# Fixed slots for the weight blocks, and another order of rounding, in the Strassen sets of an encoder's MLP

## What is computed

```python
h = _layer_norm(ALPHA * h + (mix @ w_out + b_out), ln1_g, ln1_b)
f = jnp.square(jax.nn.relu(h @ w_mlp1 + b_mlp1)) @ w_mlp2 + b_mlp2
h = _layer_norm(ALPHA * h + f, ln2_g, ln2_b)
```

## Time and profile before

| | us |
|---|---|
| median of 3 runs | 799.43 (797.58 to 800.34) |
| the profiled execution, its own time | 798.34 |
| its span | 796.6 |
| TensorE busy | 776.4 (97%) |
| VectorE busy | 519.6 (65%) |
| ScalarE busy | 426.8 (54%) |
| GpSimd busy | 145.9 (18%) |
| mean granted TensorE clock | 0.994 |

### The profile page before, as it was taken

One profiled execution on the slowest core, in us unless ns is written; L12 is line 12 of the kernel. 1 busy time (PEld: TensorE's weight loads), 2 busy tenths in 40 slices (PEclk: granted clock), 3 DMA queues, 4 the chain that ended last, 5 costly groups with the idle time before them and its releaser, 6 DMA issues.

```text
span 796.6 us, 14048 instructions
## 1 busy us (share of the span) xinstructions
PE 776.4 (97%) x5720; PEld 748.6 (94%) x5720; DVE 519.6 (65%) x762; ACT 426.8 (54%) x666; POOL 145.9 (18%) x195
## 2 busy tenths in 40 slices
PE   8999999999999999999999999999999999999995
PEld 7999899999989999999999999998999999999994
DVE  6823344754546476876968979687775887655644
ACT  5633345655646465563655556587336763477324
POOL 2100000472220110006640000000000000000356
PEclk9999999999999999999999999999999999999998
DMA  8632131112111112233112366645666456653203
GB/s 313 261 123 95 58 114 53 54 57 81 53 53 54 53 53 73 88 114 125 58 50 80 80 190 176 163 123 143 186 173 171 130 141 175 173 125 133 80 2 119
DMA packets 27070, 90.57 MB, mean 114 GB/s; under 512 B 2864, under 2 KB 7104, under 8 KB 26624
## 3 DMA queue, kind: packets, MB, share of 16 engines
q1 hardware_dynamic: 22592, 74.26, 27.3%
q0 software_dynamic: 4000, 15.10, 10.3%
q10 hardware_dynamic: 416, 0.33, 0.1%
HBM read 84.84 MB, written 4.85 MB: 113 GB/s over the span
## 4 chain that ended last, share of the span: by engine, by line
PE 80%; DVE 7%; ACT 6%; issue 3%; DMA 3%; DVEq 0%; ACTq 0%; POOL 0%; SPq 0%; POOLq 0%
PE lin L751 8%; PE lin L752 8%; PE lin L753 8%; PE z L1268 6%; PE z L1269 6%; PE z L1270 6%; PE z L1007 3%; DMA raw<-w_sets 3%; PE lin L1145 3%; PE lin L1146 3%; PE lin L1147 3%; PE lin L1285 2%; PE lin L1287 2%; PE lin L1286 2%; PE lin L1268 2%
## 5 line engine op out<-in xcount | busy, mean ns | idle before, releaser
L751 PE MATMUL lin<-h_hi,whi 128*128 128x288 f32 (+1 forms) x448 | 133.8, 299 | 0.0
L752 PE MATMUL lin<-h_lo,whi 128*128 128x288 f32 (+1 forms) x448 | 132.5, 296 | 0.0
L753 PE MATMUL lin<-h_hi,wlo 128*128 128x288 f32 (+1 forms) x448 | 132.0, 295 | 0.0
L751 PEld LDWEIGHTS lin<-h_hi,whi 128*128 128x128 f32 x448 | 84.2, 188 | 1.3 <-issue 1.1
L752 PEld LDWEIGHTS lin<-h_lo,whi 128*128 128x128 f32 x448 | 84.2, 188 | 0.1
L753 PEld LDWEIGHTS lin<-h_hi,wlo 128*128 128x128 f32 x448 | 84.3, 188 | 0.0
L1839 ACT ACTIVATE whi<-raw 128x1024 fp32r<-128x1024 f32 x48 | 50.7, 1056 | 55.4 <-DMA raw<-w_sets 18.0
L2695 DVE TENSOR_TENSOR wlo<-raw,whi 128x1024 fp32r<-128x1024 f32 x48 | 58.7, 1223 | 22.3 <-ACT whi L1839 22.3
L2098 DVE TENSOR_TENSOR wlo<-raw,whi 128x1024 fp32r<-128x1024 f32 x41 | 50.9, 1242 | 28.6 <-ACT whi L1361 26.5
L1361 ACT ACTIVATE whi<-raw 128x1024 fp32r<-128x1024 f32 x38 | 40.0, 1053 | 50.5 <-PE lin L753 32.5
L1268 PE MATMUL z<-f_ops,whi 128*128 128x288 f32 x176 | 52.8, 300 | 3.4 <-DVE f_ops L2764 2.0
(11 more groups left out here) (456 smaller groups left out, 2572.7 us busy)
## 6 DMA issues: line engine op xcount, KB each, us to landing
raw<-w_stream SPq DMA_DIRECT2D x64, 512.0 KB, 3.2
raw<-w_sets SPq DMA_DIRECT2D x48, 512.0 KB, 3.6
raw<-w_sets POOLq DMA_DIRECT2D x24, 512.0 KB, 6.9
w_fifth<-w_sets SPq DMA_DIRECT2D x12, 512.0 KB, 6.2
r<-x_t SPq DMA_DIRECT2D x8, 296.0 KB, 4.4
kcache<-k_cache SPq DMA_DIRECT2D x1, 2048.0 KB, 9.8
vcache<-v_cache SPq DMA_DIRECT2D x1, 2048.0 KB, 8.0
y<-r SPq DMA_DIRECT2D x8, 160.0 KB, 1.8
```

The lines of the kernel that those rows point to most:

```text
L751: pe.matmul(out, w_h, hi, start=first, stop=False)
L752: pe.matmul(out, w_h, lo, start=False, stop=False)
L753: return pe.matmul(out, w_l, hi, start=False, stop=last)
```

## The change

The slots no longer alternate: a, b, c, d, g are always 1, 3, 0, 2, 4. The next set's SI base goes into SI's slot as soon as SI's low part and X are made, AP's base into AP's slot behind AP's low part, AL behind DP's sum (which reads X in that slot), DE behind DP's low part, GA as before.

DP's sum moves from s2 to s3 (behind the third sum and ahead of `op_lo` of DP). ScalarE rounds V5 ahead of the next set's SI instead of behind it, and rounds B21 and T3 at s1 and V4 at s3 of the set behind, where before it rounded B21 at s0 and T3 and V4 at s1. VectorE takes V5's low part at s6 of the in set, ahead of the next set's X; V4's sum goes behind the low part of X; the low part of B21 is taken at s1, of T3 at s2, and of B22 and V4 at s4, where before B21 and T3 were at s1, B22 at s2 and V4 at s3. The low part of B11 or C11 goes behind `op_lo` at s5. In set 0 the residual operations move from s0 to s3 to s1, s2, s4 and s5.

```diff
-def set_slots(t):
-    return (1, 3, 0, 2, 4) if t % 2 == 0 else (0, 2, 1, 3, 4)
+def set_slots():
+    return 1, 3, 0, 2, 4
...
             for t in range(1, N_SETS):
-                a, b, c, d, g = set_slots(t)
+                a, b, c, d, g = set_slots()
                 o = OPS * (t - 1)
                 sp.wait_ge(s_lo, o + W_SI + 1)
                 sp.wait_ge(x_made, t)
-                load_block(t, a, 0, al_in)
-                sp.wait_ge(s_lo, o + W_X + 1)
-                sp.wait_ge(dp_made, t)
                 load_block(t, c, 2, si_base)
                 sp.wait_ge(s_lo, o + W_AP + 1)
+                load_block(t, d, 2, ap_base)
+                sp.wait_ge(dp_made, t)
+                load_block(t, a, 0, al_in)
+                sp.wait_ge(s_lo, o + W_DP + 1)
                 load_block(t, b, 1, de_in)
-                sp.wait_ge(s_lo, o + W_DP + 1)
-                load_block(t, d, 2, ap_base)
                 sp.wait_ge(s_lo, o + W_GA + 1)
                 load_block(t, g, 3, ga_in)
...
                 elif p < 3:
-                    v_hi(t, T3)
-                    v_hi(t, V4)
+                    for o in {1: (B21, T3), 3: (V4,)}.get(s, ()):
+                        v_hi(t, o)
...
                         op_hi(o + 2)
                         if SETS[tail][1] < 3:
                             v_hi(tail, V6)
-                            v_hi(tail, B21)
                         continue
...
                             block_hi(t, C12)
                         block_plain(t, C12)
+                        if p < 3:
+                            v_hi(t, V5)
                     op_hi(o + s + 2)
...
-                    if s == 1 and tail is not None:
-                        set_tail(tail, 1)
+                    if s and tail is not None:
+                        set_tail(tail, s)
...
-                    if kind == "in" and s == 6 and p < 3:
-                        v_hi(t, V5)
-                    if t == 0 and s < 4:
-                        residual2((4, 0, 2, 6)[s])
-                        residual2((5, 1, 3, 7)[s])
+                    if t == 0 and s in (1, 2, 4, 5):
+                        m = {1: 4, 2: 0, 4: 2, 5: 6}[s]
+                        residual2(m)
+                        residual2(m + 1)
...
                         if blocks:
                             last_lo(tail, C12)
-                        if sums:
-                            set_lo(tail, V5)
-                            v_sum(tail, V4)
                     if inner:
                         if s == 3:
                             third_sum(t)
                         elif s == 5:
                             fourth_sum(t)
-                            last_lo(t, C11) if p == 3 else set_lo(t, B11)
+                        elif s == 6 and p < 3:
+                            v_sum(t, V5)
+                            v_sum(t, T3)
                     elif s >= 2:
                         out_add(t, s - 2)
-                    if s == 6 and inner and p < 3:
-                        v_sum(t, V5)
-                        v_sum(t, T3)
-                    if s == 2:
+                    if s == 3:
                         dp_sum(t)
                     op_lo(o + s + 2)
...
                     if sums:
-                        for f in {0: (V6,), 1: (B21, T3), 2: (B22,), 3: (V4,)}.get(s, ()):
+                        if s == 0:
+                            v_sum(tail, V4)
+                        for f in {0: (V6,), 1: (B21,), 2: (T3,), 4: (B22, V4)}.get(s, ()):
                             set_lo(tail, f)
                     if blocks and s == 0:
                         last_lo(tail, C21)
+                    if inner and s == 5:
+                        last_lo(t, C11) if p == 3 else set_lo(t, B11)
...
                         else:
                             v_sum(t, V6)
+                            set_lo(t, V5)
                     if s == 6:
                         x_sum(t + 1)
```

More of the change, by code:

```diff
@@ L68, in sets_before, with source_slot @@
     return sum(k == kind for k, _, _ in SETS[:t])
-def set_slots(t):
-    return (1, 3, 0, 2, 4) if t % 2 == 0 else (0, 2, 1, 3, 4)
-def source_slot(t, s):
-    a, b, c, d, g = set_slots(t)
+def set_slots():
+    return 1, 3, 0, 2, 4
+def source_slot(s):
+    a, b, c, d, g = set_slots()
     return (a, c, a, b, d, b, g)[s]
@@ L689, in _ @@
             sp.wait_ge(lo_split, U_MLP1 + HIDDEN - 3)
-            load_block(0, set_slots(0)[2], 2, si_base)
+            load_block(0, set_slots()[2], 2, si_base)
             sp.wait_ge(lo_split, U_MLP1 + HIDDEN - 2)
-            load_block(0, set_slots(0)[0], 0, al_in)
+            load_block(0, set_slots()[0], 0, al_in)
             sp.wait_ge(lo_split, U_MLP1 + HIDDEN - 1)
-            load_block(0, set_slots(0)[3], 2, ap_base)
+            load_block(0, set_slots()[3], 2, ap_base)
             sp.wait_ge(lo_split, U_MLP1 + HIDDEN)
-            load_block(0, set_slots(0)[1], 1, de_in)
+            load_block(0, set_slots()[1], 1, de_in)
             sp.wait_ge(f_lo_done, F_TILES)
-            load_block(0, set_slots(0)[4], 3, ga_in)
+            load_block(0, set_slots()[4], 3, ga_in)
             for t in range(1, N_SETS):
-                a, b, c, d, g = set_slots(t)
+                a, b, c, d, g = set_slots()
                 o = OPS * (t - 1)
@@ L1838, in op_hi @@
                     act.wait_ge(op_done, o - 2)
-                nc.scalar.activation(op_home(o)[0], set_home(source_slot(t, s)), ACT.Copy).then_inc(s_hi, 1)
+                nc.scalar.activation(op_home(o)[0], set_home(source_slot(s)), ACT.Copy).then_inc(s_hi, 1)
             def first_copy(t):
@@ L2678, in x_sum @@
                     return
-                a, _, c, _, _ = set_slots(t)
+                a, _, c, _, _ = set_slots()
                 dve.wait_ge(si_in, 16 * (t + 1))
@@ L2683, in dp_sum @@
             def dp_sum(t):
-                a, b, _, _, _ = set_slots(t)
+                a, b, _, _, _ = set_slots()
                 dve.wait_ge(x_made, t + 1)
@@ L2694, in op_lo @@
                 dve.wait_ge(s_hi, o + 1)
-                tt(home[1], set_home(source_slot(t, s)), home[0].bitcast(F32), ALU.subtract).then_inc(s_lo, 1)
+                tt(home[1], set_home(source_slot(s)), home[0].bitcast(F32), ALU.subtract).then_inc(s_lo, 1)
             def out_add(t, n):
@@ L3200, in _ @@
             for t in range(N_SETS):
-                _, _, c, d, _ = set_slots(t)
+                _, _, c, d, _ = set_slots()
                 pool.wait_ge(si_base, SET_IN + 16 * (t + 1))
```

## The result

The changed kernel takes 811.91 us (811.58 to 813.04, 4 runs) against 798.96 us: a ratio of 1.0165, with an interval of 1.0144 to 1.0186. It is 13 us slower. The forecast was 809.9 us, in a range of 804 to 815. The profiled execution takes 811.58 us, its span is 809.9 us, 13.3 us more than before.

The account below looks back on a forecast made before the run. TensorE, busy for 97% of the span, was taken to bound the kernel, so only its idle time and slower stretches could change. Terms of +4.6, +6.7 and -0.8 gave +10.5 us, hence 809.9 us, range 804 to 815.

Parts of the forecast that it names:

- The sum: Whole kernel: +4.6 us for sets 2 to 5, +6.7 for sets 6 to 9, -0.8 for set 0, +10.5 us.
- Set 0: With residual operations no longer ahead of ScalarE's copy, s2 starts at 461.04 and not 461.88: 0.84 us won.
- The stalls: TensorE waits in sets 3 and 4, and likewise 7 and 8: 0.15, 1.56, 2.37, 2.38, 1.57 and 1.39 us.
- VectorE being late at s3: Set 3: lateness at s3 gives the part of the 2.4 us s6 wait above 0.6 us.
- the low end of my range: 804 us: VectorE in time at set 3's s3 saves 3.5 us in two places, smaller waits 2 us less together.
- Two of the signs: TensorE's waits for sums' low parts in sets 4 and 8 exceed 9 us; ScalarE's waits for blocks nearly vanish.
- The clock: Falls of TensorE's granted clock behind stalls in sets 3, 4, 7 and 8: taken as 0, upper end 3.4 us.
- a fall there costs nothing, since TensorE then waits anyway: Behind s6 of set 3 or s1 of set 4, a clock fall is covered by waits of 2.4 or 1.6 us.
- the 3.4 us that I had set beside it: Upper end for clock falls behind the 1.35 us stall at s5, 1.7 us each in two places.
- AL: AL, loaded behind DP's sum, lands 4 us after issue; in set 2 ScalarE wants it 4.5 us after that sum.
- Rival 2: AL lands late, at 8.8 us, delaying C22 blocks: 14 us on top, 824; chance 0.07 for more than 6 us landing.
- Rival 1: The SI block held the chain; without it sums are in time: 790.3 us, or 795 for set 4 alone; chance 0.10.

Follow-up runs that it names:

- e10: Changed kernel with the low parts of B22 and V4 moved behind the fourth sum in sets 3 and 7: 808.26 us.
- e5: Changed kernel with ScalarE's rounding of V5 put back behind the rounding of the next set's SI: 806.76 us.
- e3: Changed kernel with DP's sum put back at s2, ahead of AP's low part: 803.71 us.
- e9: Changed kernel with the base of SI for set 1 loaded ahead of GA of set 0: 810.92 us.
- e6: Changed kernel with V5's low part back behind X and V4's sum back ahead of X's low part: 811.06 us.
- e1: Kernel before with only the fixed slots and loads of the change, old order on VectorE and ScalarE: 796.25 us.
- e7: Rework of the changed kernel: slots kept, SI of set 1 early, DP's sum at s2, V5's rounding behind SI's, several low parts and sums moved: 792.33 us.
- e4: Changed kernel with the low part of B22 back at s2 and that of V4 back at s3: 806.58 us.
- e2: Changed kernel with the old alternating slots and loads, new order on VectorE and ScalarE kept: 816.32 us.

## Why the prediction was right

**The sum.** 10.5 us were forecast and 13 measured, with an interval of 11.5 to 14.9. For sets 2 to 5 and 6 to 9 the forecast was 76.6 us each; measured 76.64 and 76.60. Set 0 was to win 0.84 us and won 0.7.

**The stalls.** At s2 of set 3, 1.56 forecast and 1.52 measured (as distance between matmuls over 0.133 us); at s6, 2.37 and 2.35; at s1 of set 4, 2.38 and 2.41; at s5, 1.39 and 1.37. At s4 of set 3 none was forecast and none came. e10 and e5 confirm two of the parts of which they were made: 1.3 us for two low parts, 1.1 us for the order of V5's and SI's rounding.

The stall at s6 of set 3 had its size right and its parts wrong. I had put 0.6 us of it down to the new order there and the rest to VectorE being late at s3. In e5 TensorE waits 0.9 us less at s2 and the stall at s6 is still 2.35 us; from s2 to s6 it is 15.22 us (530.62 to 545.84), in the changed kernel 15.23 (531.97 to 547.20). So the lateness of set 3's start gives nothing of it, and the 3.5 us that it took off for the low end of my range are a saving that no run shows. What e3 and e10 show in its place is DP's sum at s3, without which there is no stall at all, and on top of it the two low parts.

Two of the signs came only in part. TensorE's waits for the sums' low parts grew to 6.9 us and not to over 9, since a fall of the clock filled the time of the wait at s2 of sets 4 and 8 (below). And ScalarE's waits for blocks fell from 24.6 to 7.9 us, but that for SI of set 1 (4.5 us) stayed, which points at the set that I left out.

**The clock.** A fall came behind s1 of sets 4 and 8, none at s6. At s2 of set 4, where 1.57 us of stall were forecast, the changed kernel shows 0.04: the fall took the stall's place. e3, which has a stall of 2.4 us at s1 as well but no fall, shows what that place costs without one:

```profile
552.56 0.37 PE L1267 MATMUL z<-f_ops,whi 128*128 128x288 f32 x1 [2.23 <-DVE f_ops L2763]
...
557.39 0.37 PE L1267 MATMUL lin<-f_ops,third_hi 128*128 128x288 f32 x1 [1.44 <-DVE f_ops L2763]
```

4.83 us from s1 to s2 in e3, 4.82 in the changed kernel (556.05 to 560.87). e10 has both in one execution: behind s1 of set 4 no fall and behind s1 of set 8 one (the column ahead of the last two), and the sets take 27.68 and 27.71 us.

```profile
555.50:558.50 3.00, 2.87 (x22) 2.64 (x21) 1.87 (x3) 2.50 (x4) 0.00 (x0) 1.00 0.50 164
...
653.50:656.50 3.00, 3.00 (x15) 3.00 (x14) 2.15 (x3) 3.00 (x5) 0.00 (x0) 0.50 0.54 175
```

So the step "a fall there costs nothing, since TensorE then waits anyway" holds. It holds for s6 too: in e9 the clock falls behind s6 of sets 3 and 7, and the pairs take 54.3 and 54.2 us, as in the changed kernel (54.3 and 54.3), which has no fall there. The rule of the Trainium skill's page "TensorE: Matmul & The Clock Gate", section "What's actually happening", by which the sets with more idle time show more falls, agrees with the count, two over the MLP for one before; the 3.4 us that I had set beside it did not come, since both were free. e6 shows that they cost some 1.4 us each once nothing covers them.

**The step that was missing: set 1.** I worked out sets 0, 3, 4, 7 and 8 and put set 1 at nothing without writing its queue down. It lost 2.3 us: 0.35 and 0.21 us at s1 and s2, where SI's block is late, and 1.34 us at s6, for the fourth output add (the row for L2712). In set 1 VectorE also has four low parts of 1.35 us for the normed input. With them, the adds and a hole of 1.13 us for DP's rounding its queue is longer than TensorE's. Two rows of VectorE in set 1 of the changed kernel show such a low part and the hole:

```profile
487.67 1.35 DVE L2780 TENSOR_TENSOR hs_lo<-hs_sums,hs_hi 128x1152 fp32r<-128x1152 f32 x1
...
491.95 1.23 DVE L2694 TENSOR_TENSOR third_lo<-raw,third_hi 128x1024 fp32r<-128x1024 f32 x1 [1.13 <-ACT third_hi L1838]
```

In e3, with DP's sum at s2 (and SI 1 us less late), the wait is gone; e9 shows that an early SI removes most of it. This is nearly all of the 2.5 us between forecast and result.

**AL.** It was to land 4 us behind its issue; in set 2 DP's sum ended at 513.24 and AL was rounded from 518.31, 5.1 us. Rival 2 was to decide from 5.3 us on, and it did not, though by 0.2 us only. The Trainium skill, "DMA: Bandwidth & Descriptors", section "Queues, rings and completion order", has each DMA engine alternate between the queues with work; the trace agrees in so far as this load, with POOL's accumulate of AP issued at 514.56 beside it, takes more than the 3.1 us that a load can take. The slack was enough.

**Rival 1**, the intended gain, is right about a part of it: e1 shows that the SI block did hold the chain, and taking it off is worth 1.5 us with its stall and its fall of the clock. It went wrong where the forecast said, in two low parts ahead of the fourth sum and a rounding ahead of SI, and most of all in DP's sum at s3 (e3).

## What to carry to other kernels

Where two engines hand a block to and fro, put work of the first engine into the time in which the second rounds: a sum directly ahead of the operand made from it (e3), or a rounding directly behind the sum that it waits for (e5), opened a hole as long as the other engine's step, and in this kernel everything behind paid for it. An operation for which TensorE waits soon goes ahead of one that is needed a set later, even if both fit the engine's total load; VectorE was 64% busy in the changed kernel and 66% in e7. And a load that is made earlier may be worth little alone, 1.5 us here: write down what stands behind it in the same queue for every set, also for the one that looks like its neighbours.

## What the runs showed of the hardware that was not expected

A stall's length does not say whether the clock falls behind it. Behind a stall of 2.4 us at s1 of sets 4 and 8 it fell in the changed kernel both times, in e3 neither time, and in e4 and e10 in set 8 and not in set 4, within one execution. Behind the stall of 2.35 us at s6 of set 3 it fell in e9 and e2 and not in the changed kernel and e5, and behind the same stall in set 7 it fell in e5 as well. Behind stalls of 2.0 us it fell in the kernel before and in e6. Nor does the stall ahead of it decide: in e10 TensorE had waited 1.02 us at s6 of set 3 and 1.03 us at s6 of set 7. What does decide stays open.

The price of a fall was 0 where TensorE had to wait behind it in any case, an estimate of 1.4 us in e6, and some 1.3 us in the kernel before. There the same product of set 8 stands behind a stall too, a shorter one with no fall:

```profile
644.41 0.37 PE L1268 MATMUL z<-f_ops,third_hi 128*128 128x288 f32 x1 [1.14 <-DVE f_ops L2764]
```

From there to set 9 it is 663.83 - 644.41 = 19.42 us, and from the same product of set 4 to set 5 571.69 - 550.99 = 20.70 us.
